# A residual network on one Trainium2 core: the order of a few VectorE and ScalarE instructions at three hand-overs to the matrix engine

## What is computed

```python
def short_conv_mixer(proj, conv_w, w_out):           # the conv layer
    bg, cg, xt, g = jnp.split(proj, 4, axis=-1)      # proj = h @ odd_w_in, 1024 x 4096
    u = cg * xt
    up = jnp.pad(u, ((0, 0), (1, 1), (0, 0)))
    conv = sum(conv_w[t] * up[:, t:t + n] for t in range(3))
    return (bg * conv * jax.nn.silu(g)) @ w_out

def conv_ffn(x, w_in, conv_w, conv_b, w_out):        # the feed-forward layer
    h = causal_depthwise_conv(x @ w_in, conv_w, conv_b)    # 1024 x 5632, three taps
    val, gate = jnp.split(h, 2, axis=-1)
    return (jax.nn.silu(gate) * val) @ w_out         # 2816 x 1024
```

## Time and profile before

| what | us |
|---|---|
| median of 3 runs | 1866.57 |
| lowest and highest | 1864.5, 1866.86 |
| profiled execution, its own time | 1863.36 |
| its span in the profile | 1861.5 |
| PE busy in it | 1773.5 (95%) |
| DVE, ACT, POOL busy | 1165.7, 802.6, 753.1 |
| mean granted TensorE clock (1.0 is full speed) | 0.983 |

### The profile page before, as it was taken

How to read it: one execution, slowest core, us unless ns; L and a number is a source line. 1 busy time by engine, 2 the same in 40 slices (tenths; PEclk the granted TensorE clock), 3 DMA queues, 4 the chain that set the end, 5 groups by cost and what they waited for, 6 DMA issues and landing times.

```text
span 1861.5 us, 22926 instructions
## 1 busy us (share of the span) xinstructions
PE 1773.5 (95%) x8745; PEld 1475.9 (79%) x8745; DVE 1165.7 (63%) x1312; ACT 802.6 (43%) x1246; POOL 753.1 (40%) x451
## 2 busy tenths in 40 slices
PE   5899999889999699999999999999999999999999
PEld 3688888658888578878888888987888888878887
DVE  3703975338988642865454553487666666679876
ACT  5324221346666622643333342645444344444443
POOL 0325222000000023266666531256999999920000
PEclk9899999899999999999999999999999999999999
DMA  8413112550000180212222341312222323187433
GB/s 323 148 51 114 46 57 91 201 198 1 0 0 1 42 287 34 68 57 79 69 72 64 107 165 46 88 49 68 80 91 80 90 80 91 57 302 266 139 120 123
DMA packets 162088, 188.31 MB, mean 101 GB/s; under 512 B 9230, under 2 KB 117319, under 8 KB 160839
## 3 DMA queue, kind: packets, MB, share of 16 engines
q1 hardware_dynamic: 161991, 187.00, 30.4%
HBM read 152.37 MB, written 34.60 MB: 100 GB/s over the span
## 4 chain that ended last, share of the span: by engine, by line
PE 53%; DVE 3%; ACT 2%; issue 1%; DMA 1%; POOL 0%; SPq 0%; ACTq 0%; DVEq 0%; POOLq 0%
PE ps L2993 18%; PE ps L1991 14%; PE ps L3044 11%; PE ps L2051 5%; PE ps L2003 1%; PE ps L3344 1%; PE ps L3006 1%; PE ps L2007 1%; DVE up_lo_p L130 1%; DVE residual L2863 0%; DMA res_scratch<-x_nat 0%; PE ps L3010 0%; ACT residual L3180 0%; DVE residual L2902 0%; DMA y_a<-y_scratch 0%
## 5 line engine op out<-in xcount | busy, mean ns | idle before, releaser
L2993 PE MATMUL ps<-up_hi_p,st_hi_p 128*128 128x512 f32 x560 | 218.0, 389 | 3.4 <-ACT residual L2711 3.4
L2993 PE MATMUL ps<-up_hi_p,st_lo_p 128*128 128x512 f32 x560 | 217.9, 389 | 0.0
L2993 PE MATMUL ps<-up_lo_p,st_hi_p 128*128 128x512 f32 x560 | 217.9, 389 | 0.0
L3044 PE MATMUL ps<-down_ring 128*128 128x512 f32 x924 | 210.7, 390 | 2.4 <-DVE down_ring L130 2.3
L3044 PEld LDWEIGHTS ps<-down_ring 128*128 128x128 f32 x924 | 173.0, 188 | 39.9 <-issue 4.2
L130 POOL TENSOR_TENSOR in_lo<-in_raw,in_hi 128x512 fp32r<-128x512 f32 (+1 forms) x56 | 92.9, 1666 | 230.6 <-ACT in_hi L127 180.9
L1991 PE MATMUL ps<-cv_hi_p,cv_st_hi_p 128*128 128x512 f32 x392 | 153.2, 391 | 2.5 <-ACT residual L1709 2.5
L1991 PE MATMUL ps<-cv_lo_p,cv_st_hi_p 128*128 128x512 f32 x392 | 153.2, 391 | 0.0
L1991 PE MATMUL ps<-cv_hi_p,cv_st_lo_p 128*128 128x512 f32 x392 | 153.0, 390 | 0.0
L130 POOL TENSOR_TENSOR st_lo_p<-up_raw,st_hi_p 128x512 fp32r<-128x512 f32 x68 | 100.9, 1487 | 67.2 <-ACT st_hi_p L127 67.2
L2993 PEld LDWEIGHTS ps<-up_hi_p,st_hi_p 128*128 128x128 f32 x560 | 105.1, 188 | 26.1 <-issue 3.4
(11 more groups left out here) (373 smaller groups left out, 4206.2 us busy)
## 6 DMA issues: line engine op xcount, KB each, us to landing
up_raw<-in_ffn_w_in SPq DMA_DIRECT2D x44, 512.0 KB, 5.1
w_raw<-in_ffn_w_out SPq DMA_DIRECT2D x66, 256.0 KB, 3.0
ada_raw_rest<-in_ada_w SPq DMA_DIRECT2D x32, 512.0 KB, 6.2
cv_raw<-in_odd_w_in SPq DMA_DIRECT2D x32, 512.0 KB, 5.4
in_raw<-in_even_w_in SPq DMA_DIRECT2D x48, 256.0 KB, 2.7
y_scratch<-residual SPq DMA_DIRECT2D x22, 512.0 KB, 2.6
ada_raw<-in_ada_w SPq DMA_DIRECT2D x8, 1024.0 KB, 17.4
residual<-in_x SPq DMA_DIRECT2D x2, 2048.0 KB, 10.5
```

The lines of the kernel that those rows point to most:

```text
L2993: last = pe.matmul(ps[:, bank(j, p), :], w[p][:, kk * P:(kk + 1) * P], x[p][:, kk, :], start=(first and w is st_hi and x is up_hi), stop=( ...
L3044: last = pe.matmul(ps[:, 4 * (i % 2) + m, :], slot[:, s, m * P:(m + 1) * P], slot[:, x, :], start=(k == 0 and s == 0 and x == 2 and DOWN[i ...
```

## The change

Nothing is added or removed: the instructions stay the same on every engine, and some stand elsewhere.

- Conv layer, ACT: `p1_copy(2)` stands ahead of the four `plain_out` of the second group instead of behind `middle_tap(0)`. It waits for `gated_input(0)`, whose input it overwrites. `middle_tap(0)` gets a wait for the last low of the differences.
- Conv layer, DVE: `gated_input(0)` stands ahead of step 3's differences.
- Feed-forward layer, ACT: `p1_copy(2)` stands ahead of `ga_tap2(0)`.
- Down phase, ACT: `high_pair(4)` and `high_pair(5)` stand ahead of `ga_tap2(21)`.
- Down phase, DVE: `low_t(4)`, `low_s(5)` and `low_t(5)` stand ahead of `ga_taps(21)`.

```diff
@@ -1780,13 +1780,16 @@
                     high_stationary(act, p, 2)
                 for p, kk in DIFFS[10:]:
                     difference_high(p, kk)
+                p1_copy(2)
                 for kind, side in PLAIN_OUT:
                     plain_out(1, kind, side)
                 for p in ("p3", "p4"):
                     high_stationary(act, p, 2)
+                moving_stands(act, "p4", HALF - 1)
                 middle_tap(0)
                 for g in range(2, G - 1):
-                    p1_copy(g)
+                    if g > 2:
+                        p1_copy(g)
                     high_stationary(act, "p1", g + 1)
                     high_stationary(act, "p6", g + 1)
                     if g % 2 == 0:
@@ -1950,8 +1953,8 @@
                 differences(1)
                 combine_next(dve, 2)
                 differences(2)
+                gated_input(0)
                 differences(3)
-                gated_input(0)
                 tap_before(0)
                 tap_after(0)
                 for g in range(2, G):
@@ -2784,8 +2787,8 @@
                     difference_high(p, kk)
                 for kind, side in PLAIN_OUT[:2]:
                     plain_out(1, kind, side)
+                p1_copy(2)
                 ga_tap2(0)
-                p1_copy(2)
                 for kind, side in PLAIN_OUT[2:]:
                     plain_out(1, kind, side)
                 for p in ("p3", "p4"):
@@ -2811,10 +2814,11 @@
                 for t in range(SLOTS):
                     high_pair(act, t)
                 va_tap2(N - 1)
+                high_pair(act, SLOTS)
+                high_pair(act, SLOTS + 1)
                 ga_tap2(N - 1)
-                high_pair(act, SLOTS)
                 silu(N - 1)
-                for t in range(SLOTS + 1, N_STEPS):
+                for t in range(SLOTS + 2, N_STEPS):
                     high_pair(act, t)
 
             def ffn_pool(pool):
@@ -2962,16 +2966,19 @@
                     if j == N - 1:
                         low_t(dve, 3)
                     c21(j)
+                low_t(dve, SLOTS)
+                low_s(dve, LOW_FIRST)
+                low_t(dve, LOW_FIRST)
                 ga_taps(N - 1)
-                low_t(dve, SLOTS)
                 product(N - 1)
                 for t in range(LOW_FIRST, N_STEPS):
                     if HALF_N <= t + 2 < N_STEPS:
                         combine_s(dve, t + 2)
                     if 2 * HALF_N <= t + 3 < N_STEPS:
                         combine_t(dve, t + 3)
-                    low_s(dve, t)
-                    low_t(dve, t)
+                    if t > LOW_FIRST:
+                        low_s(dve, t)
+                        low_t(dve, t)
                     if t < HALF_N:
                         for k in (2 * (t - LOW_FIRST), 2 * (t - LOW_FIRST) + 1):
                             if k < HALF_N:
```

## The result

Twenty runs of each kernel, on the same chips: the changed kernel takes 1868.31 us (median, 1864.11 to 1872.43), the kernel before 1864.97 (1858.5 to 1868.59). The ratio of the two is 1.0020, with a 95% interval of 1.0011 to 1.0029: 3.7 us slower, between 2.1 and 5.4. The forecast was 1867.3 and "no change", with a sum of +0.7. So the time lies in the range and the change brings nothing, as predicted. But it costs 0.2%, and that is clear of the noise: the interval of the difference leaves out +0.7, and the sum was 3 us short.

What follows compares the result with a forecast made beforehand. PE bounds the kernel, with 8.2 us of waits at the moved instructions and about 10 us at stake. Terms +1.6 - 0.1 - 0.8 = +0.7 took the median from 1866.57 to 1867.3 us, range 1863.8 to 1870.0.

Steps and rivals of the forecast that it cites:

- a sum of +0.7: Whole kernel: conv layer +1.6, feed-forward layer -0.1 and down phase -0.8 us, taken as no change.
- Conv wait: Conv layer, third group: the 2.5 us wait goes, but PE waits 4.5 us at p4 for c22.
- Clock price of the conv wait: Conv layer, behind p4's new wait: 1.4 us lost to low clock, bounds 0 and 1.7.
- Rival 2: Whole kernel slower by low clock behind the new gaps: +4.2 us, 1870.8; chance 0.07.
- Its second half: Feed-forward layer: low clock behind the gap at p1_copy(3) costs 1.65 us, with nothing to hide it.
- its own sign: Whole kernel: the slower-by-clock case decides once more than 9 us of PE's work run at 0.50.
- The credit for the old clock loss: Conv layer: p4 starts about 815.8 against 815.61 before, which includes 1.65 us of low-clock loss; 0.2 later.
- Feed-forward layer: Third group: PE waits 2.2 us for c22 at p4, then 1.6 at p1_copy(3); layer -0.1 us.
- a low clock behind the first gap would be hidden by the second: Feed-forward layer: 1.65 us of clock loss behind p4's wait fits in 1.6 us of slack at p1_copy(3).
- Down phase: Step 6 waits 1.4 us, step 10 starts earlier; phase -0.8 us, gain bounds 0.1 and 1.4.
- the issue and the landing come 0.7 to 0.8 earlier: Down phase: the y_a22 load is issued and lands 0.7 to 0.8 us earlier, so step 10 gains 0.8.
- My own bound for that case: Down phase: a gain of 0.1 us if the y_a22 transfer lands when it did.

Runs made afterwards that it cites:

- conv_chain: Changed kernel, conv third group on DVE: u2 and the next group's sums ahead of the taps, u4 and c22 right behind; ratio 0.9977 to the kernel before.
- ffn_only: Kernel before with only the feed-forward layer's p1_copy(2) moved; ratio 0.9994 to the kernel before.
- tap_first: Changed kernel with ACT's conv middle_tap(0) ahead of the four bank copies and two highs; ratio 1.0025 to the kernel before.
- ffn_chain: Changed kernel, feed-forward third group: DVE's u2, u4 and c22 earlier, ACT's two highs and p1_copy(3) ahead of silu(1); ratio 1.0026 to the kernel before.
- down_only: Kernel before with only the down-phase part of the change; ratio 1.0013 to the kernel before.
- all_chain: Changed kernel with conv_chain's and ffn_chain's orders, the y_a22 load issued early and step 6's lows ahead of the combine_t pair; ratio 0.9978 to the kernel before.
- best: Changed kernel with all_chain's conv and down orders and a second feed-forward order on DVE and ACT; 1855.37 us, ratio 0.9962 to the kernel before.
- down_load: Changed kernel with SP's first y_a22 load issued ahead of the last y store and weights 8 to 10; ratio 1.0008 to the kernel before.
- conv_only: Kernel before with only the conv part of the change; ratio 1.0031 to the kernel before.
- store_late: Changed kernel with SP's last y store issued behind weights 8 to 10 and the first y_a22 load; ratio 1.0029 to the kernel before.

## Why the prediction was right, and where its sizes were off

**Conv wait: right.** The copy just in time, p4 next and 4.5 us long, `middle_tap(0)` at 8.17 behind the group's start (802.8 - 794.9 = 7.9 predicted), p4 0.34 later than in the first profile of before (0.2 predicted). What the prediction left out is POOL beside `gated_input(0)`; it used up the 0.2 us that the copy had to spare. conv_chain shows the cause by removing it.

**Clock price of the conv wait: mis-sized.** The step that failed is "Bounds 0 and 1.7; I take 1.4, since 4.5 is nearest to 4.1" (with these bounds the conv layer's upper end is 1.9, not the 2.1 given). It was 2.8, outside the bounds, in the changed kernel; and 6.8 us of low clock stood behind this wait in seven profiles of seven (4.1 to 4.5 us long). The nearest row, the wait of 4.1 us, was one sample. Rival 2 named this size (3.3), with a chance of 0.07, and the part of it that was right is this one. Its second half, low clock that counts at `p1_copy(3)`, did not come: the low clock came behind p4 of the feed-forward layer, where the slack took it up. By its own sign, more than 9 us of PE's work at 0.50, it was just met (5.8 us behind the one wait and 3.4 behind the other), and its +4.2 is nearer to the measured 3.7 than the forecast's +0.7.

**The credit for the old clock loss: one profile taken for a property.** The 0.2 between the two starts of p4 is counted from the first profile's 815.61, which has 1.65 us of low clock in it. Three other profiles don't have it. Conv layer: forecast +1.6, measured +3.1 against the first profile and +4.4 against the other three.

**Feed-forward layer: right.** 2.2 us predicted at p4, 2.0 measured; -0.1 predicted for the layer, -0.11 measured, and in ffn_only -0.13. That a low clock behind the first gap would be hidden by the second is what the trace shows, and ffn_only, without low clock, comes to the same.

**Down phase: mis-sized, with the wrong sign.** The wait of 1.4 before step 6 came (1.14 in the row, 1.3 with the slower first matmul). The step that failed is "the issue and the landing come 0.7 to 0.8 earlier": the issue did, the landing didn't. My own bound for that case was a gain of 0.1, and even that was not reached. The phase takes 212.80 to 213.02 us in the four profiles that have the part with nothing else changed in the phase and no low clock (the changed kernel, tap_first, conv_chain, ffn_chain), 215.04 in down_only, and 211.61 to 212.73 in the four without it. Instead of -0.8: +0.15 against the first profile, +0.6 against the mean of the four (212.29).

**Sum.** +3.1 - 0.1 + 0.15 is 3.2, and the medians differ by 3.3. That this fits so well is partly luck: against the other profiles of before the conv stage alone is +4.4, and the stretch between the layers adds up to 4 us of time, with 10.2 us more of low clock. That stretch has 6.8 to 13.7 us of low clock in all ten profiles with a changed conv stage, those without a wait among them, and 3.4 in three of four with the old one.

The granted clocks of all executions speak against 4 us that always come there. The span times what the clock lacks to 1.0 is the time lost to low clock. In the six other kernels with the long wait at p4 it is on average 1.9 to 4.2 us more than in the kernel before of the same round (10 or 12 executions against 17 to 35; the standard error of each difference is 1.2 to 2.0 us). The windows behind p4 in the two layers alone make about 4 (2.8 and 1.6, less 0.4 for the one in four of before). In conv_chain, all_chain and best the difference is -1.4, +0.9 and -4.3. This is an estimate with a wide error; why single profiles differ so in that stretch, no run settled.

**Luck in the time.** The change itself measured +3.3, above the +2.3 that the forecast's terms allow. The time lies in the range, 1.0 us from the forecast, because the kernel before, run twenty times, has a median 1.6 us below the 1866.57 of three runs from which the forecast was counted, and because the range had 1.1 us added at each end.

## What to carry to other kernels

Before an operand is moved ahead for an engine that waits, look for the next operand it will need and move that one's chain too: here the consumer's own order on DVE (c22 ahead of two products that nobody waited for) was worth 7.4 us with the low clock that went, and the copy alone less than nothing. A wait's price in clock can't be read from one row; take several executions or keep its whole spread in the range. An earlier issue is not yet an earlier landing: here a load issued 1.06 us earlier was used no earlier. Issue it far ahead, as down_load does, or don't count the gain.

## What the runs showed of the hardware

- Behind PE waits of 4.1 to 4.5 us the granted clock was at 0.50 for 6.8 us in seven profiles of seven; behind 2.5 to 2.7 us in the same layer for 3.4 us in one of four; behind 2.0 us at p4 of the feed-forward layer in five profiles of seven; behind the 3.0 us at its p2 in one of four (conv_only, whose layer is 0.8 us longer for it).
- Between the two layers the kernel before ran with 13.7 us of low clock in one profile and 3.4 in another; over all kernels, which share this code, it was 3.4 to 13.7.
- A DVE sum of 128x512 takes 0.68 us alone and 1.66 to 1.78 beside a POOL low, a tap 1.28 and mostly 2.1 to 2.3 (1.70 in one place of the changed kernel), the 128x1024 product of the gated input 1.22 and 2.31: the collision costs DVE up to 1.1 us each time, whichever instruction it hits.
- The y_a22 load was used 5.6 to 5.8 us after its issue in four profiles without the down part and 6.7 to 7.5 in five with it, with the same order in SP's queue; 7.3 in store_late.
